# Gate and up as one 256-column product in the expert blocks of a mixture of experts, with relays by halves of k

## What is computed

```python
D_EXPERT, N_EXPERTS, TOP_K_EXPERTS = 512, 16, 2

def run_block(args):
    e, toks = args
    xb = x_pad[toks]
    h = jax.nn.silu(xb @ w1[e]) * (xb @ w3[e])
    return h @ w2[e]

yb = lax.map(run_block, (blk_e, slot_tok.reshape(n_blk, MOE_BLOCK)))
y = yb.reshape(-1, D) * slot_gate[:, None]
return jnp.zeros((N + 1, D), x2.dtype).at[slot_tok].add(y)[:N]
```

## Time and profile before

| what | value |
|---|---|
| median of 3 runs | 3313.47 us (3309.04 to 3322.31) |
| span of the profiled execution | 3333.5 us |
| PE busy | 94% of the span |
| PE's share of the chain that ended last | 88% |
| DVE, ACT, POOL busy | 58%, 26%, 13% |
| DMA queue q1, which carries the weights | 381.70 MB |
| first and last start of an `up` product (L1094) | 653.9 and 1949.7 us, in two stretches of about 305 us |

### The profile page before, as it was taken

The page is one execution under the profiler, slowest core; times in us unless marked ns, Lnnn a source line. Parts: engine busy times, 40 slices in busy tenths (PEclk is TensorE's granted clock), DMA queues, the critical chain, the costliest instruction groups (busy, mean ns, idle before and its releaser), DMA issues.

```text
span 3333.5 us, 73560 instructions
## 1 busy us (share of the span) xinstructions
PE 3119.7 (94%) x28638; PEld 2349.2 (70%) x28639; DVE 1931.1 (58%) x3792; ACT 873.4 (26%) x1559; POOL 422.1 (13%) x345
## 2 busy tenths in 40 slices
PE   8998999799988998999699979999999899999997
PEld 5445887577765445886577748888778578588886
DVE  1476574456641575664555657664576656476644
ACT  1116110356632116110456641000022522110000
POOL 1000000322222000000322210000055133000000
PEclk9999999899999999999899989999999999999998
DMA  7110323389952110323389942222334000122231
GB/s 284 63 64 1 127 89 146 126 322 377 380 215 92 52 62 14 127 89 152 124 334 375 375 158 86 89 89 89 103 96 107 25 2 3 62 79 87 89 99 66
DMA packets 83202, 443.23 MB, mean 133 GB/s; under 512 B 19480, under 2 KB 19616, under 8 KB 39336
## 3 DMA queue, kind: packets, MB, share of 16 engines
q1 hardware_dynamic: 56488, 381.70, 31.5%
q0 software_dynamic: 23568, 55.62, 4.6%
q10 hardware_dynamic: 2928, 3.07, 0.3%
HBM read 411.00 MB, written 29.23 MB: 132 GB/s over the span
## 4 chain that ended last, share of the span: by engine, by line
PE 88%; ACT 4%; issue 4%; DVE 3%; DVEq 1%; DMA 0%; POOL 0%; ACTq 0%; POOLq 0%
PE pb L1223 24%; PE pb L788 12%; PE pb L1094 11%; PE pb L955 9%; PE pb L1117 5%; PE pb L995 4%; PE pb L1337 4%; PE pb L1049 3%; PE pb L1604 2%; ACT arena L1632 1%; PE pb L824 1%; PE pb L892 1%; PE pb L935 1%; PE pb L1101 1%; ACT xT L1662 1%
## 5 line engine op out<-in xcount | busy, mean ns | idle before, releaser
L1223 PE MATMUL pb<-arena,streamed 128*128 128x256 f32 x1952 | 446.6, 381 | 3.6 <-DVE arena L2496 2.8
L1223 PEld LDWEIGHTS pb<-arena,streamed 128*128 128x128 f32 x1952 | 372.6, 191 | 56.8 <-ACT xT L1662 3.2
L1094 PE MATMUL pb<-streamed,xT 128*32 128x128 f32 x9024 | 358.9, 276 | 11.5 <-issue 11.3
L1094 PE MATMUL pb<-arena,xT 128*32 x3008 | 353.3, 276 | 16.1 <-issue 10.2
L788 PE MATMUL pb<-xT,streamed 128*128 128x512 f32 x832 | 367.8, 600 | 0.0
L1094 PEld LDWEIGHTS pb<-arena,xT 128*32 128x32 f32 x3008 | 322.9, 111 | 30.6 <-issue 24.5
L1094 PEld LDWEIGHTS pb<-streamed,xT 128*32 128x32 f32 x9024 | 327.9, 111 | 15.9 <-issue 15.8
L788 PEld LDWEIGHTS pb<-xT,streamed 128*128 128x128 f32 x832 | 159.4, 193 | 200.9 <-issue 200.8
L1758 ACT ACTIVATE streamed<-arena 128x3072 f32 x94 | 260.2, 2768 | 56.1 <-remote 37.5
L1223 PE MATMUL pb<-arena,am 128*128 128x256 f32 x976 | 227.3, 379 | 0.0
L1117 PE MATMUL pb<-arena,am 128*32 x3008 | 193.7, 391 | 23.4 <-issue 18.5
(11 more groups left out here) (497 smaller groups left out, 5393.0 us busy)
## 6 DMA issues: line engine op xcount, KB each, us to landing
arena<-in_w_moe SPq DMA_DIRECT2D x192, 1024.0 KB, 9.6
streamed<-in_w_tail SPq DMA_DIRECT2D x87, 1024.0 KB, 5.0
streamed<-in_w_layer SPq DMA_DIRECT2D x78, 1024.0 KB, 4.9
xT<-xs_dram POOLq DMA_DIRECT2D x22, 512.0 KB, 8.4
ys_dram<-xT POOLq DMA_DIRECT2D x88, 128.0 KB, 9.1
xs_dram<-lnw POOLq DMA_DIRECT2D x12, 512.0 KB, 18.8
arena<-rel_dram SPq DMA_DIRECT2D x8, 448.0 KB, 9.4
lnw<-in_ln_par POOLq DMA_DIRECT2D x3, 1024.0 KB, 6.8
```

What stands on the lines that cost most here:

```text
L1094: last = mm(pb[m][r0:r0 + MOE_BLOCK, 0:FW], rows, w, start=(k == 0), stop=(k == KC - 1))
L1223: last = mm(pb[p][:, 0:HALF], stat(i), mov(i), start=(opens and i == 0), stop=(closes and i == steps - 1))
```

## The change

`up(b)` makes gate and up in one product: for one k and one quarter the moving operand is 2 x 128 columns, w1's beside w3's, and the result goes to one bank, gate in columns 0 to 127 and up in 128 to 255. The relays are cut by k and no longer by matrix: the front (k 0 to 3 of both, by DVE) and the back (k 4 to 7 of both, by ACT). `up_ready` is now given after k 3 and after k 7. `gate_half` waits for the second, `relay_front` for the first. DVE makes `relay_front(b + 1)` ahead of `hidden(b)`. SP loads pieces 0 and 2, then 1 and 3, then 4 and 5. On PE the place of the block before step 1 is carried over the loop's edge in a register, instead of being read again.

```diff
+        PARTS = ((0, 2), (1, 3), (4, 5))
+        def both(at, k):
+            return arena[:, bass.ds(at + k * D_EXP, UP_PIECES * PAIR)].rearrange("p (m n) -> p m n", m=2)
+        def of_expert(at, first):
+            w = arena[:, bass.ds(at, UP_PIECES * PAIR)].rearrange("p (m k c) -> p m k c", m=2, k=KC)
+            return w[:, :, first:first + KC // 2, FW:D_EXP]
...
-        w1_relay, w3_relay = streamed[:, 0:RELAY], streamed[:, RELAY:2 * RELAY]
+        up_relay = streamed[:, 0:2 * RELAY].rearrange("p (m k c) -> p m k c", m=2, k=KC)
...
-                        load(e, 2 * m)
-                        load(e, 2 * m + 1)
+                        for p in PARTS[m]:
+                            load(e, p)
...
-                    for m, (relay, relayed) in enumerate(((w1_relay, w1_relayed), (w3_relay, w3_relayed))):
+                    for half, relayed in enumerate((front_relayed, back_relayed)):
                         pe.wait_ge(relayed, l * N_BLK + b + 1)
                         alone(pe)
-                        for k in range(KC):
+                        for k in range(half * KC // 2, (half + 1) * KC // 2):
+                            rows = xsT[:, k * P + s % COLS * MOE_BLOCK:k * P + (s % COLS + 1) * MOE_BLOCK]
                             for g in range(COLS):
                                 r0 = g * MOE_BLOCK
-                                rows = xsT[:, k * P + s % COLS * MOE_BLOCK:k * P + (s % COLS + 1) * MOE_BLOCK]
-                                w = arena[:, bass.ds(off + (m * KC + k) * D_EXP, FW)] if g == 0 else relay[:, (k * (COLS - 1) + g - 1) * FW:(k * (COLS - 1) + g) * FW]
-                                last = mm(pb[m][r0:r0 + MOE_BLOCK, 0:FW], rows, w, start=(k == 0), stop=(k == KC - 1))
+                                w = both(off, k)[:, :, 0:FW] if g == 0 else up_relay[:, :, k, (g - 1) * FW:g * FW]
+                                last = mm(cut(pb[0][r0:r0 + MOE_BLOCK, 0:2 * FW], FW), rows, w, start=(k == 0), stop=(k == KC - 1))
                         last.then_inc(up_ready, 1)
...
+                pe.reg_mov(slot_before, slot(0))
                 with pe.Fori(0, N_TILE - 1) as i:
+                    off = pe.snap(slot_before, min_val=0, max_val=SLOT)
                     for s in range(1, COLS + 1):
                         b = i * COLS + s
                         ahead = slot(b)
                         up(b, s, ahead, i + s // COLS)
-                        if s == 1:
-                            off = slot(b - 1)
...
+                    pe.reg_mov(slot_before, ahead)
...
-                def relay_w1(b, e):
-
-                    act.wait_ge(expert_here[0], l * N_EXP + e + 1)
+                def relay_back(b, e):
+
+                    act.wait_ge(expert_here[1], l * N_EXP + e + 1)
                     alone(act)
-                    fn(cut(w1_relay, D_EXP - FW), cut(arena[:, bass.ds(slot_of(e), KC * D_EXP)], D_EXP)[:, :, FW:D_EXP], ACT.Copy).then_inc(w1_relayed, 1)
+                    fn(up_relay[:, :, KC // 2:KC], of_expert(slot_of(e), KC // 2), ACT.Copy).then_inc(back_relayed, 1)
...
-                    act.wait_ge(up_ready, 2 * (l * N_BLK + b) + 3)
+                    act.wait_ge(up_ready, 2 * (l * N_BLK + b) + 4)
...
+                def relay_front(b, e):
+
+                    dve.wait_ge(expert_here[0], l * N_EXP + e + 1)
                     alone(dve)
+                    if b:
+                        dve.wait_ge(up_ready, 2 * (l * N_BLK + b - 1) + 3)
+                        alone(dve)
+                    v.tensor_copy(up_relay[:, :, 0:KC // 2], of_expert(slot_of(e), 0)).then_inc(front_relayed, 1)
...
-                    dve.wait_ge(up_ready, 2 * (l * N_BLK + b) + 4)
-                    alone(dve)
                     dve.wait_ge(sil_ready, l * N_BLK + b + 1)
                     alone(dve)
-                    v.tensor_tensor(hid, pb[1][:, 0:FW], sil, ALU.mult).then_inc(hid_ready, 1)
+                    v.tensor_tensor(hid, pb[0][:, FW:2 * FW], sil, ALU.mult).then_inc(hid_ready, 1)
...
+                    if b + 1 < N_BLK:
+                        relay_front(b + 1, ahead)
                     hidden(b)
                     if b == 0:
                         dve.wait_ge(last_turned, l + 1)
                         alone(dve)
-                    if b + 1 < N_BLK:
-                        relay_w3(b + 1, ahead)
```

More of the change, by code:

```diff
@@ L230, in gate_diagonal, with part_of @@
             return pw_b[:, at:at + P]
+        PARTS = ((0, 2), (1, 3), (4, 5))
+        def part_of(p):
+            return p % 2 if p < UP_PIECES else 2
+        def both(at, k):
[3 more added lines that the diff above has]
+            return w[:, :, first:first + KC // 2, FW:D_EXP]
         def piece(e, p):
@@ L343, in two_blocks @@
         xs_loaded = sem("xs_loaded")
-        expert_loaded = [sem(f"expert_loaded_{n}") for n in ("w1", "w3", "w2")]
-        expert_here = [sem(f"expert_here_{n}") for n in ("w1", "w3", "w2")]
-        w1_relayed, w3_relayed, w2_relayed = sem("w1_relayed"), sem("w3_relayed"), sem("w2_relayed")
+        expert_loaded = [sem(f"expert_loaded_{n}") for n in ("front", "back", "down")]
+        expert_here = [sem(f"expert_here_{n}") for n in ("front", "back", "down")]
+        front_relayed, back_relayed, w2_relayed = sem("front_relayed"), sem("back_relayed"), sem("w2_relayed")
         xs_tr, xsT_ready = sem("xs_transposed"), sem("xsT_ready")
@@ L479, in copies_used @@
                 if s < 2:
-                    sp.wait_ge(up_ready, 2 * layers * N_BLK + 1 + s)
+                    sp.wait_ge(up_ready, 2 * layers * N_BLK + 2)
                 else:
@@ L501, in load @@
                     sp.dma_start(piece(e, p), a["w_moe"][bass.ds((l * N_EXP + e) * PIECES + p, 1)]
-                                 .rearrange("a p n -> p (a n)")).then_inc(expert_loaded[p // 2], 16)
+                                 .rearrange("a p n -> p (a n)")).then_inc(expert_loaded[part_of(p)], 16)
                 def arrived(e, m):
@@ L521, in _ @@
                 load(1, 0)
+                arrived(0, 1)
                 load(1, 1)
-                arrived(0, 1)
                 load(1, 2)
@@ L528, in _ @@
                 arrived(0, 2)
-                load(1, 4)
-                load(1, 5)
+                for p in PARTS[2]:
+                    load(1, p)
                 sp.wait_ge(route_ready, l + 1)
@@ L771, in _ @@
             mm = nc.tensor.matmul
+            slot_before = pe.alloc_register("slot_before")
             def pair(j, l=None, i=0, per=1):
@@ L1796, in _ @@
                 alone(act)
-                relay_w1(0, block_expert(act, 0))
+                relay_back(0, block_expert(act, 0))
                 fn(primed, ones[:, 0:1], ACT.Silu)
@@ L1804, in _ @@
                     if b + 1 < N_BLK:
-                        relay_w1(b + 1, e)
+                        relay_back(b + 1, e)
                     if b == 0:
@@ L2369, in _ @@
                 v.tensor_copy(blk_tab[:, :], r_tab).then_inc(route_ready, 1)
-                def relay_w3(b, e):
-                    dve.wait_ge(expert_here[1], l * N_EXP + e + 1)
+                def relay_front(b, e):
+                    dve.wait_ge(expert_here[0], l * N_EXP + e + 1)
                     alone(dve)
-                    v.tensor_copy(cut(w3_relay, D_EXP - FW), cut(arena[:, bass.ds(slot_of(e) + 2 * PAIR, KC * D_EXP)], D_EXP)[:, :, FW:D_EXP]).then_inc(w3_relayed, 1)
+                    if b:
+                        dve.wait_ge(up_ready, 2 * (l * N_BLK + b - 1) + 3)
+                        alone(dve)
+                    v.tensor_copy(up_relay[:, :, 0:KC // 2], of_expert(slot_of(e), 0)).then_inc(front_relayed, 1)
                 dve.wait_ge(route_ready, l + 1)
@@ L2380, in _ @@
                 e = block_expert(dve, 0)
-                relay_w3(0, e)
+                relay_front(0, e)
                 v.tensor_tensor(r_t, r_pick, r_score, ALU.mult)
```

## The result

| kernel | median, us | lowest to highest | ratio to before |
|---|---|---|---|
| before, 6 runs beside it | 3317.59 | 3309.04 to 3325.76 | |
| changed, 6 runs | 3343.48 | 3340.71 to 3360.61 | 1.0088 (95% interval 1.0067 to 1.0109) |

The change makes the kernel 0.9% slower, by 26 us. The forecast was 3346 us. The profiled execution of the changed kernel has a span of 3341.0 us.

The account below looks back on a forecast made before the run. PE bounds the kernel (88% of the span), with the row copy and hidden chains lacking slack. Per round -0.25 - 0.84 + 0.99 + 1.77 = +1.67; 35 + 1 + 2 - 5 = +33, so 3346 us, range 3318 to 3368.

Parts of the forecast that it names:

- Width: PE's up: 16 groups of 256 columns take 3.47 us against 3.51 for 32 of 128; -0.25 us per round.
- rival of cheaper wide products: PE's up: a 256-column group takes only 0.13 us, 5.6 us less a round, about 3292 us; chance 0.05.
- The 1.2: Estimated price of a 256-column matmul relative to 128, by which each up would fall by about 40%.
- The slot read: PE after up of step 1: no longer reading the previous block's place saves 0.84 us per round.
- Hidden later: Product of gate and up on DVE starts 0.33 us late, delaying the next up in three steps; +0.99 us per round.
- The row copy: ACT's copy of the transposed rows, queued behind the relay, moves by 1.77 us and delays up of step 4; +1.77 per round.
- The slack that the forecast gave the back relay: ACT's back relay ends at D + 3.61, needed at D + 3.72 by the next up's second half; hidden by 0.1.
- code: First blocks, PE issue waits on code run for the first time: up has half the instructions; -5 us, bounds 0 and -10.
- Around the loop: Blocks outside the loop: +1 us from four cases of about +0.3, +2 from relay_front(6) going ahead of hidden(5).
- The relays' form: Relay copies as two runs of 1536: pace kept; rival has DVE falling to ACT's pace, 94 us more, about 3440, chance 0.03.
- the ceiling of the transfers: Transfers reach at best 394 GB/s, so no round under 23.96 us and gains stop near -22 us.
- two rivals: Row copy and hidden not late, or wide products cheaper: each held to about 3292 us, chance 0.05 each.

Follow-up runs that it names:

- e4: Kernel before with only the register that carries the previous block's place instead of reading it again, products still 128 columns: 3305.66 us, ratio 0.9962.
- e3: Changed kernel with the place of the block before read again after up of step 1, without the register: 3338.37 us, ratio 1.0056.
- e5: Changed kernel with the row copy on DVE and the next block's place read ahead of turn, both places in registers: 3285.67 us, ratio 0.9911.
- e7: Changed kernel with DVE's old order, hidden ahead of the front relay: 3404.28 us in one run.
- e1: Changed kernel with ACT's row copy placed ahead of the back relay: 3314.11 us, ratio 0.9982.
- b0: Kernel before, unchanged, profiled once more: 3317.96 us, span 3315.7.
- e2: Changed kernel with the row copy made by DVE between hidden and relay_w2, none on ACT: 3308.65 us, ratio 0.9970.
- e6: Kernel before with both places in registers and the next place read ahead of turn, 128-column products: 3301.85 us, ratio 0.9953.

## Why the prediction was right

**Width.** Forecast -0.25 a round; each `up` came out at 3.47 instead of 3.51, so -0.16 or so, which is what the forecast's own 16 x 0.217 gives. This settles the rival of cheaper wide products: a group of 256 columns takes 3.47/16 = 0.217. With float32 and 32-column weights the ratio to the 0.110 of 128 columns is 2. The 1.2 that the prediction estimated between two figures of the Trainium skill ("TensorE: Matmul & The Clock Gate", Back-to-back issue gap), which has none for 256 columns, does not show here.

**The slot read.** Forecast -0.84; `up` 1 to `down` fell by 0.81, of which 0.04 is width. The size was right. The cause was put down too narrowly, to the register: e4 shows that the register alone brings it, e3 that the wide products alone bring it too. The two gains do not add up.

**Hidden later.** Forecast 0.80 behind `down` and +0.99 a round; it was 0.76, and the three steps lost 0.31, 0.26 and 0.27, together +0.84. e5 shows that the chain from `hidden` over the sequencer is what PE waited for, since shortening it without touching `hidden` gives the time back. e7 shows that the silu decides where `hidden` starts. The front relay, of which the forecast took the earliest end that it had, 0.68 after `down`, ended 0.74 after it in the block shown and so had nothing to spare either.

**The row copy.** Forecast +1.77, `up` 4 at 4.9 to 5.0; measured +1.75, at 4.95. e1 takes it away by order alone. The slack that the forecast gave the back relay in an ordinary block (0.1) was there: `up` is 3.47 everywhere in the changed kernel.

**Sum and the rest.** Forecast +1.67 a round, rounds of 26.6; measured +1.60, 26.59. For code -5 was forecast, and the first blocks became 5.1 shorter although they carry late terms too; that it is for fewer instructions was argued, not shown. Around the loop +3 was forecast, and the table has +2.9 behind the rounds, but that is luck, since the two do not cover the same work. The +2.9 holds the last row copy of each layer, which the forecast had in its rounds: `up` starts 5.76 and 4.95 us after these transposes, and 3.20 in b0. It lacks block 5, in which the forecast had 2 of its 3; that block is in the first of the 20 rounds. And the last `up` of each layer, which took 4.53 and 4.66 us in b0, takes 3.47 in the changed kernel, which the forecast did not have.

Forecast +33 in all, +25.3 in the spans and +26 in the medians. Of the 8 between +33 and the spans 5 are in the expert blocks (+33 forecast, +28.1 in the three stretches of them) and 3 in all the rest, for which the forecast had nothing. The absolute figure came nearer than this by luck: the median of before that stood beside the forecast, 3313.47, was 4 lower than in the later runs. With 3317.59 it would have said 3351, 7 over the 3343.48.

**The relays' form.** DVE's two runs of 1536 take 1762 ns, ACT's 2767: as before. This agrees with the rule that the forecast cited of the Trainium skill ("VectorE: DVE Perf Modes", What auto-detection actually checks). No run here had a form by which the rule would make this copy slower, so it is not tested further.

**What was wrong** is the ceiling of the transfers, a step of two rivals: I took 394 GB/s for the most, and so no round under 23.96. e5 has rounds of 23.77 at 403. The highest rate seen in a kernel that asks for no more is no bound.

## What to carry to other kernels

When a trigger is merged with a later one, follow everything that stands behind it in its engine's queue: the wide product cost nothing on PE, and most of what was lost came from a copy of 1 us that stood behind a relay of 2.8 us, as before, when the trigger of both came 1.75 us later. A queue with nothing to spare does not show in the list of waits; it shows where the gap behind it is exactly the latency from semaphore to work. Before adding the gains of two edits, ask whether both remove the same wait, and move what an engine's sequencer has to read ahead of the wait at which it stands, not behind.

## What was not expected of the hardware

The stores that POOL issues (`ys_dram`) take different times in kernels in which POOL does the same work. In the window of 700 to 900 us, of before, of the changed kernel and of e5 (count, busy us, mean ns):

```profile
L644 POOL DMA_DIRECT2D ys_dram<-xT x32 | 43.1, 1346 | 125.8 <-ACT xT L1793 120.6 <-issue 5.3
```

```profile
L659 POOL DMA_DIRECT2D ys_dram<-xT x30 | 23.3, 776 | 152.7 <-ACT xT L1810 148.5 <-issue 4.2
```

```profile
L659 POOL DMA_DIRECT2D ys_dram<-xT x34 | 54.2, 1594 | 140.4 <-ACT xT L1813 136.0 <-issue 4.5
```

It was 1068 in e1, 820 in e2, 774 in e3, 1454 in e4, 1449 in e6 and 856 in e7. The length of the rounds does not order them: e5 with 23.77 us has long ones, but so has the kernel before with 25, while e2 with 24.77 has short ones. What orders them is where DVE's relays fall. A store that none is in the way of takes 0.69 to 0.71 us, as this one of the changed kernel:

```profile
705.10 0.69 POOL L659 DMA_DIRECT2D ys_dram<-xT  x1 [6.70 <-ACT xT L1810]
```

This one of e5 starts just ahead of a front relay. The relay ends at 705.36 and the store at 705.62, 0.26 later:

```profile
703.34 2.28 POOL L659 DMA_DIRECT2D ys_dram<-xT  x1 [8.26 <-ACT xT L1813]
703.60 1.76 DVE L2396 COPY streamed<-arena 128x3072 f32 x1 [0.44 <-PE pb L1111]
```

The same holds for all longer stores that start in this window, in all ten profiles: 197 take more than 0.71 us, and each of them ends 0.25 or 0.26 us after the end of a front relay or of a copy of the w2 relay. That copy had begun by 0.27 us after the store's start and was still running 0.53 after it. The other 118 take 0.69 to 0.71. In 48 of them no copy of DVE ran at all, and in the rest it was over by 0.36 us after the store's start or began no sooner than 0.38 after it. In the two profiles of before, in e4 and in e6 every store meets a copy of the w2 relay, so there is not one short store. An issue on POOL that meets such a copy thus lasts until the copy has ended. This is read from the times, and no kernel was run to try it. POOL was never late for PE in this window.
